# Transposing the gated product of a feed-forward network on VectorE and by transfers instead of on TensorE

## The reference, cut to what matters

```
a, b = split(h @ w_ffn_in)        # w_ffn_in 2048 x (2 * 5632)
x = x + (silu(a) * b) @ w_ffn_out # w_ffn_out 5632 x 2048
```

## Time and profile before

| | us |
|---|---|
| median of 3 runs | 2570.8 (2570.18 to 2571.73) |
| the profiled execution | 2571.48 |
| its span, first to last instruction | 2569.7 |
| TensorE busy | 2553.4 (99%) |
| VectorE busy | 1861.1 (72%) |
| ScalarE busy | 1233.7 (48%) |
| transfer engines, share of the span | 70.3% for the queue of SyncE |

### The profile page before, as it was taken

How to read it: one execution, slowest core, us unless ns; L and a number is a source line. 1 busy time by engine, 2 the same in 40 slices (tenths; PEclk the granted TensorE clock), 3 DMA queues, 4 the chain that set the end, 5 groups by cost and what they waited for, 6 DMA issues and landing times.

```text
span 2569.7 us, 33931 instructions
## 1 busy us (share of the span) xinstructions
PE 2553.4 (99%) x11820; PEld 2126.1 (83%) x11820; DVE 1861.1 (72%) x2418; ACT 1233.7 (48%) x1491; POOL 18.7 (1%) x28
## 2 busy tenths in 40 slices
PE   9999999999999999999999999999999999999998
PEld 7888888888888888888888888888888888888887
DVE  6777767666457676767777776885698777777786
ACT  6545456554554444444444545555644444444443
POOL 0000000000000000000000000000000000000000
PEclk9999999999999999999999999999999999999999
DMA  8876767676658777877778587774577776667665
GB/s 312 281 249 210 228 208 241 197 240 219 189 181 266 257 254 250 255 254 254 255 251 255 176 254 229 225 223 150 166 226 225 219 216 221 215 216 220 212 218 180
DMA packets 281444, 584.30 MB, mean 227 GB/s; under 512 B 17968, under 2 KB 28384, under 8 KB 280432
## 3 DMA queue, kind: packets, MB, share of 16 engines
q1 hardware_dynamic: 279376, 574.25, 70.3%
q0 software_dynamic: 1952, 8.49, 1.1%
HBM read 580.54 MB, written 2.13 MB: 227 GB/s over the span
## 4 chain that ended last, share of the span: by engine, by line
PE 93%; DVE 3%; DMA 2%; ACT 1%; issue 1%; SPq 0%; DVEq 0%; ACTq 0%
PE acc L1275 81%; PE W L1275 10%; DMA raw<-in_w_in 2%; DVE wlo L1775 1%; PE W L1355 1%; ACT whi L620 1%; PE W L1492 0%; PE acc L1630 0%; DVE raw L1788 0%; DVE rr L2067 0%; DMA raw<-in_w_ada_t 0%; DVE arena L1840 0%; ACT hHL L670 0%; DVE arena L1939 0%; DVE hHL L1848 0%
## 5 line engine op out<-in xcount | busy, mean ns | idle before, releaser
L1775 DVE TENSOR_TENSOR wlo<-raw,whi 128x1024 fp32r<-128x1024 f32 x888 | 1082.8, 1224 | 656.6 <-ACT whi L620 652.8
L620 ACT ACTIVATE whi<-raw 128x1024 fp32r<-128x1024 f32 x888 | 937.2, 1059 | 1145.6 <-PE acc L1275 889.7
L1275 PE MATMUL acc<-whi,hHL 128*128 128x512 f32 x4992 | 1245.8, 391 | 4.2 <-issue 2.1
L1275 PEld LDWEIGHTS acc<-whi,hHL 128*128 128x128 f32 x4992 | 932.3, 188 | 197.6 <-issue 5.7
L1275 PE MATMUL acc<-wlo,hHL 128*128 128x512 f32 x2496 | 669.0, 389 | 0.0
L1275 PEld LDWEIGHTS acc<-wlo,hHL 128*128 128x128 f32 x2496 | 468.5, 188 | 98.4 <-DVE wlo L1775 0.4
L1788 DVE CUSTOM_DVE_ANT_0 raw<-raw,crow 128x1024 f32<-128x1024 f32 x192 | 234.0, 1219 | 5.2 <-DMA raw<-in_w_ada_t 5.2
L1275 PE MATMUL acc<-whi,yH 128*128 128x512 f32 x768 | 209.4, 394 | 0.0
L1275 PE MATMUL acc<-wlo,yH 128*128 128x512 f32 x768 | 205.5, 389 | 0.0
L1275 PE MATMUL acc<-whi,yL 128*128 128x512 f32 x768 | 205.5, 389 | 0.0
L1275 PEld LDWEIGHTS acc<-whi,yL 128*128 128x128 f32 x768 | 144.2, 188 | 30.3
(11 more groups left out here) (221 smaller groups left out, 1077.1 us busy)
## 6 DMA issues: line engine op xcount, KB each, us to landing
raw<-in_w_in SPq DMA_DIRECT2D x264, 512.0 KB, 4.7
raw<-in_w_ada_t SPq DMA_DIRECT2D x192, 512.0 KB, 4.7
raw<-in_w_ffn_in SPq DMA_DIRECT2D x176, 512.0 KB, 4.5
raw<-in_w_up SPq DMA_DIRECT2D x128, 512.0 KB, 4.3
raw<-in_w_down SPq DMA_DIRECT2D x128, 512.0 KB, 4.5
raw<-in_w_ffn_out SPq DMA_DIRECT2D x88, 512.0 KB, 4.9
raw<-in_w_out SPq DMA_DIRECT2D x32, 512.0 KB, 4.4
raw<-in_w_o SPq DMA_DIRECT2D x32, 512.0 KB, 4.1
```

The lines of the kernel that those rows point to most:

```text
L620: act.activation(whi[:, v], raw[:, s], ACT.Copy).then_inc(S("w_hi"), 1)
L1275: return pe.matmul(o, l, r, start=start, stop=stop, skip_group_check=True)
L1775: dve.tensor_tensor(wlo[:, v], raw[:, s], whi[:, v].bitcast(F32), ALU.subtract)\
```

## The change

In the first network TensorE no longer transposes. After the second `gated`, VectorE's new `bank_turn` transposes the tile in two instructions, one for each half of the tokens, over all 128 partitions and 512 columns. VectorE transposes 32x32 blocks only within their 32 partitions, so the result (`banked`) has each block turned but still on the partitions of its tokens. Sixteen transfers (`move`), each 32 partitions by 256 columns, SBUF to SBUF, bring the blocks to the partitions of their features (`gated_turned`). SyncE issues them four at a time behind the loads of units 8, 9, 10 and 11 of the next pass (for the last tile, eight ahead of and eight behind the first load of the last `down1`). ScalarE makes the high part after nine units of the pass instead of four, VectorE the low part after ten. TensorE's `turn_act`, its waits and its hook are gone.

```diff
+            def move(b, n):
+                for i in range(b, b + n):
+                    sp.dma_start(bank(gated_turned, i % 4, i // 4), bank(banked, i // 4, i % 4)).then_inc(S("ff_moved"), 16)
+
             def ffn1(i, down):
...
                     for u in range(8):
                         load(wv["w_ffn_in"][:, u * KU:(u + 1) * KU, ds(i * GCOL + half * D_FF1, GCOL)])
+                        if down and half and u == 0:
+                            sp.wait_ge(S("ff_bank"), i)
+                        if down and half and u < 4:
+                            move(4 * u, 4)
...
             pl.leave(10, 32, 0, 0, 1)
+            sp.wait_ge(S("ff_bank"), 11)
+            move(0, 8)
             for g in range(4):
...
                     load(wv["w_ffn_out"][:, group_k + u * KU:group_k + (u + 1) * KU, g * GCOL:(g + 1) * GCOL])
+                    if g == 0 and u == 0:
+                        move(8, 8)
...
+            def product_hi(q):
+                act.activation(in_banks(yH[:, q]), by_bank(gated_turned), ACT.Copy).then_inc(S("ff_hi"), 1)
...
-                    hi(); hi(); hi(); hi()
-                    act.wait_ge(S("ff_turn"), n)
-                    act.wait_ge(S("w_used"), pl.v + pl.ov - 4)
-                    act.activation(yH[:, 0:GT], tiles(turned), ACT.Copy).then_inc(S("ff_hi"), 1)
-                    hi(); hi(); hi(); hi()
+                    for _ in range(9):
+                        hi()
+                    act.wait_ge(S("ff_moved"), n * 256)
+                    act.wait_ge(S("w_used"), pl.v + pl.ov - 9)
+                    product_hi(slice(0, GT))
+                    for _ in range(3):
+                        hi()
...
-            def turn_act(n):
-                pe.wait_ge(S("ff_act"), n)
-                turn(tokens(act32[:, 0:1024]), turned, "ff_turn")
-
...
-                    if g == 2 and not last:
-                        turn_act(n + 1)
...
+            def bank_turn(src, dst, ready, sem):
+                dve.wait_ge(S(ready[0]), ready[1])
+                for t in range(TT):
+                    x = tokens(src)[:, t].rearrange("p (m j f) -> p j m f", j=4, f=32)
+                    ins = dve.transpose(dst.rearrange("p (j m t c) -> p t j m c", j=4, t=TT, c=32)[:, t], x)
+                ins.then_inc(S(sem), 1)
...
-                if down:
-                    dve.wait_ge(S("ff_turn"), n)
                 gated(tokens(act32[:, 0:1024]), acc[:, (PHASES["ffn1"][1] + 1) % 2], "ff_act")
+                bank_turn(act32[:, 0:1024], banked, ("ff_act", n + 1), "ff_bank")
```

More of the change, by code:

```diff
@@ L296, in tokens, with by_bank, in_banks, bank @@
             return ap.rearrange("p (t n) -> p t n", t=TT)
+        def by_bank(ap):
+            return ap.rearrange("p (a k c) -> p k a c", a=4, c=32)
+        def in_banks(y):
+            return y.rearrange("p m (t a c) -> p (m t) a c", t=TT, c=32)
+        def bank(x, i, j):
+            return x[32 * i:32 * i + 32, j * 256:(j + 1) * 256]
         def cols(ap, c):
@@ L313, in build @@
         DOWN = [Wf[:, 0:2 * GCOL], Wf[:, 2 * GCOL:], UP[0], UP[1]]
+        banked = act32[:, 1024:2048]
+        gated_turned = blk(8)[:, 0:1024]
         act_turned = [blk(10)[:, h * 1024:(h + 1) * 1024] for h in range(2)]
@@ L983, in ffn1 @@
                     pl.phase("ffn1")
-                    hi(); hi(); hi(); hi()
-                    act.wait_ge(S("ff_turn"), n)
-                    act.wait_ge(S("w_used"), pl.v + pl.ov - 4)
-                    act.activation(yH[:, 0:GT], tiles(turned), ACT.Copy).then_inc(S("ff_hi"), 1)
-                    hi(); hi(); hi(); hi()
+                    for _ in range(9):
[5 more added lines that the diff above has]
+                        hi()
                 else:
-                    for _ in range(begin, 8):
+                    for _ in range(begin, 12):
                         hi()
-                for _ in range(4):
-                    hi()
                 if not down:
@@ L1008, in _ @@
             pl.leave(10, 32, 24, 6, 1)
-            act.wait_ge(S("ff_turn"), 11)
-            act.activation(yH[:, GT:], tiles(turned), ACT.Copy).then_inc(S("ff_hi"), 1)
+            act.wait_ge(S("ff_moved"), 11 * 256)
+            product_hi(slice(GT, 2 * GT))
             for _ in range(8):
@@ L1615, in _ @@
             ffn1(0, (("x1", 3), ("x1", 4)), False, hooks={1: lambda: turn_x1(3)})
-            ffn1(1, (("ff_g", 1), ("ff_act", 1)), True, hooks={1: lambda: turn_act(1)})
+            ffn1(1, (("ff_g", 1), ("ff_act", 1)), True)
             with pe.Fori(0, 9) as i:
@@ L2233, in product_low @@
                 dve.wait_ge(S("ff_hi"), n)
-                dve.tensor_tensor(yL[:, q], tiles(turned), yH[:, q].bitcast(F32), ALU.subtract).then_inc(S("ff_lo"), 1)
+                dve.tensor_tensor(in_banks(yL[:, q]), by_bank(gated_turned), in_banks(yH[:, q].bitcast(F32)), ALU.subtract)\
+                   .then_inc(S("ff_lo"), 1)
+            def bank_turn(src, dst, ready, sem):
[4 more added lines that the diff above has]
+                ins.then_inc(S(sem), 1)
             def add_down(g, n, v):
@@ L2252, in ffn1 @@
                     add_down(3, n - 1, here() - 4)
-                    product_low(n)
                     lo(4)
                 else:
-                    if down:
[L2257 to L2261, removed]
+                    lo(8 - begin)
                 def gated(dst, a, sem):
@@ L2267, in gated @@
                     ins.then_inc(S(sem), 1)
-                lo(4)
+                lo(2)
+                if down:
+                    product_low(n)
+                lo(2)
                 dve.wait_ge(S("ff_sig"), n + 1)
```

## The result

The changed kernel takes 2627.7 us (median of 4 runs, 2624.1 to 2629.5); the kernel before, on the same chip, 2571.3. The ratio is 1.0218 (95% interval 1.0205 to 1.0231): 56.4 us slower, where 3.6 slower was predicted and 2587 was the end of the range. The profiled execution took 2629.5 us.

A forecast was written before the change was run, and what follows sets the result against it. TensorE, busy nearly all of the span and 93% of the chain, was taken as the bound. Turns -9.8, new wait +9.6, later lag +3.0, last tile +0.8 gave +3.6 us on median 2570.8: 2574.4 us, range 2562.5 to 2587.

The forecast's parts named there:

- What bounds the kernel, and the turns: TensorE bounds the loop; removing eleven turns of 0.89 us from its path gains 9.8 us.
- VectorE's transposes: Two a pass behind the second gated product, 0.75 us each, with 6.8 us to spare and nothing on the path.
- The moves' issue: On SyncE's queue, issues back to back are 0.51 us apart, so four moves hold it 1.6 to 2.0 us.
- the next two sets fit between the loads of units 9, 10 and 11: On SyncE's queue, three issues in 5.81 us leave room, so the load of unit 11 stands at 842.92.
- The new wait: At unit 9, ScalarE waits for moves landing behind the `w_ada_t` load; TensorE stalls 0.96 us a pass, 9.6 us.
- Rival 1: Moves behind unit 11 land by their own latency, 2.1 us; stall under 0.3 us, 2562 to 2565 us; chance 0.2.
- What is late next: After unit 9, the 4.7 us lag at unit 12 is just used up by the next unit 8; 3 us allowed.
- Rival 2: Lag isn't made up by next unit 8: `whi` 8 late by 0.7 to 1.5 us, 2578 to 2587 us; chance 0.3.
- The last tile: Ahead of the last `down1`, two sets of eight moves hold the queue 3.3 to 4.1 us each; 0.8 us cost.

The follow-up runs named there:

- e7: e1 without the last tile's moves: 2561.7 us, ratio 0.9961.
- e5: The changed kernel with only the last four of the sixteen moves in each pass, four for the last tile, ScalarE waiting for these: 2604.6 us, ratio 1.0122.
- e14: e7 without any move, ScalarE making eight idle copies between `whi` 8 and the product's high part: 2605.1 us, ratio 1.0125.
- e9: e5 with VectorE's second gated product one unit earlier, ahead of `wlo` 19: 2608.1 us, ratio 1.0142.
- e1: The changed kernel with all sixteen moves issued, but the product made from the block-turned tile without waiting for them: 2569.0 us, ratio 0.9993.
- e11: The changed kernel with 9 extra 128-column products on TensorE behind unit 8 of each pass: 2622.6 us, ratio 1.021.
- e12: e1 with 20 extra 128-column products on TensorE ahead of the last `down1`: 2567.3 us, ratio 0.9985.

## Why the prediction was wrong, step by step

**What bounds the kernel, and the turns.** Right. Eleven turns were put at 9.8 us, e7 gives 9.6, and its pass of 65.28 us is 66.17 less 0.89.

**VectorE's transposes.** Right, 0.75 us each predicted and nothing on the path:

```profile
L2266 DVE STREAM_TRANSPOSE arena<-arena 128x512 f32<-128x512 f32 x18 | 11.7, 690 | 0.3
```

**The moves' issue.** Wrong in size: 0.51 us apart at most, 1.6 to 2.0 for four. They take 2.41 for four and 0.63 apart. That looks small, but the step "the next two sets fit between the loads of units 9, 10 and 11" rests on it: 2.41 and 0.38 and the gaps make 3.1 us, over the 2.72 of a unit. Load 11 is 2.3 us late and the `w_ada_t` load behind it takes 1.47 us to issue instead of 0.34. The issues of 0.47 were taken for the upper end, but they are of another shape: a row of 0.5 us for something else isn't a bound.

**The new wait.** The mechanism was right: in every pass of e5 but one, and in every pass of the changed kernel, the last move lands 0.6 to 0.8 us behind the `w_ada_t` load ahead of it (0.4 was taken), whether that load takes 4.6 or 6.4 us. So was its size for what it described: e5, with just the last four moves, stops 1.2 us at unit 9 in the median (1.35 in the mean) against 0.96. In the whole change the last move lands 10.8 to 12.4 us after `whi` 8 starts instead of 9.06, by the step above, and the stop is 2.9.

```profile
arena<-arena SPq DMA_DIRECT2D x160, 32.0 KB, 3.3
```

Rival 1 (moves land by their own latency, in 2.1 us) is false: 3.3 us in the median, 2.1 to 4.3. Even 2.1 would not have saved it, since the last is issued 8.2 us after `whi` 8 starts (9.3 in the pass shown), and to be in time it had to land 8.1 us after it. The short landing exists, but not there: the last four moves of the last tile, issued when the load ahead of them was nearly or fully in, land in 1.8 to 1.9 us:

```profile
L498 SPq DMA_DIRECT2D arena<-arena x4: 590/590/592, 1468.1 to 1470.0; - x4
...
DMA to landing us min/median/max: 1.8/1.8/1.9
```

**What is late next.** This is the step that failed, and it holds most of the error: 3.0 us for all passes, where e5 loses about 3.2 us in each. Two things in it were wrong. First, the lag isn't made up at 0.8 to 1.0 us in three units, but at about 0.4: in e5 `whi` 12 to 14 start some 5.7 us behind their places at 2.72 us a unit, `whi` 21 to 23 still 4.5. The landings aren't the reason; the loads of the loop take 4.8 us in the mean before and after. `wlo` shares VectorE with dot products, gated products, transposes and sums, but which of them uses up the circle wasn't tried. Second, I took the four-unit lead of the weights for the cover everywhere. At units 18 and 20 it isn't. There TensorE waits for an accumulator that VectorE empties behind `wlo` 19 (unit 18) and `wlo` 21 (unit 20), so the cover is what those had to spare, 1.4 us at unit 18. A lag of 4.7 us at unit 12 that shrinks slowly comes out there as a stop. The row to look for was in the profile of before: the end of the second gated product (807.82) beside the start of unit 18 (809.20). e14 shows this without transfers, e9 shows that these waits stand in a row so that freeing one hands the stop to the next. The four stops of e5 together (4.6 us) are as long as the lag that is left at the end of its pass (4.5).

Rival 2, "the lag isn't made up", has the right name but not what happened. Its condition, an average landing of 5.2 us, didn't come (4.8), and neither did its sign: in all passes of the changed kernel `whi` 8 still waits for TensorE and starts 14.02 us after unit 0, as before. The lag is gone by then because TensorE has paid for it at units 18, 20 and 22. Forecast and rival both looked only at `whi` 8 of the next pass; that place came out as forecast, by another path. The rival's price was 1.6 to 2.5 us a pass; the changed kernel's passes cost 6.1 us over the 65.28 (71.4 in the mean).

**The last tile.** 0.8 predicted, 7.4 measured (e1 less e7). The two sets of eight were put at 3.3 to 4.1 us each and take 4.95; and I asked when the product would be ready, not when the next loads would go out between and behind the moves. The load behind the second eight leaves at 1410.3 in e1 and its `whi` ends at 1416.2, TensorE's weight loads being done at 1413.0; then come its `wlo` and the sum that TensorE waits for. It is the hand-over of units 18 and 20 once more.

**The clock.** It wasn't in the sum. In or behind most of the longer stops TensorE was granted 1.2 GHz for 3.41 or 6.83 us. In the loop this cost up to about 1 us a pass (e11), at the last tile about 2 us (e12).

## What to carry to other kernels

When a step makes an engine late, don't stop at the first unit that it hits: list every hand-over in the rest of the pass (weights, accumulators, slots), read the time to spare of each from the trace, and compare it with the lag that is left there; the smallest one decides, not the longest lead. Price small transfers by the time they take from the queue that issues them, and where that is the queue of the critical loads, place them where nothing waits, or let an idle engine issue them (here +2.9 us by the place alone, -4.4 from GpSimd, instead of +56.4 for the same moves). A load queue that is faster than TensorE by a few tenths of a microsecond in three units can't make up a delay of 5 us within a pass.

## What the runs showed of the hardware

- A 32 KB transfer from SBUF to SBUF (32 rows of 1 KB) holds SyncE's queue 0.5 to 0.6 us, longer than a 512 KB load of weights (0.34 to 0.38). The Trainium skill, "DMA: Bandwidth & Descriptors", section "Rules for kernel authors", says that below 64 KB one pays mostly overhead; the trace agrees: a sixteenth of the bytes of a weight load lands in 3.3 us against 4.6 to 5.2. On GpSimd the same issue took 498 ns.
- Small moves take 3.3 us to land between weight loads, and 1.8 us where the load ahead is in or nearly in. The last of a set of four lands 0.6 to 0.8 us behind the load issued ahead of it (once 1.9); the first move of a set can land before that load (1463.76 against 1465.31 ahead of the last `down1`).
- Back to back with moves, a load's own issue went from 0.34 to 1.47 us.
- The granted clock fell at some stops and not at others of like length: in the changed kernel not at 2.69 us (786.9) and 2.60 us (1146.2), but at 2.48 us (932.3) and 2.42 us (1359.7). In the first network it fell at each stop of 2.84 us and more in the traces of these kernels. A stretch at 1.2 GHz began up to 3.1 us before TensorE started again (e11) and up to 1.3 us after (e5). What tells the stops apart wasn't tried.
- Half the clock behind a stop costs less than it slows where the next units wait anyway: of at most 18.8 us some 5 came back by the medians, some 10 by the profiled passes (e11), the first not clear of noise.
